# A relative-bias table fetched in two transfers over 128 partitions instead of four over 64

## What is computed

```python
GRID_W = 64; N_HEADS = 16; WIN_ROWS = 8; WIN_COLS = 16     # 128 latent tokens are 2 rows of 64

def na_latent(h, ctx_k, ctx_v, wqkv, wo, rpb):
    ...                                                    # R = 2 grid rows, KR = 2
    row_b = (row_idx - r[:, None]) + (WIN_ROWS - 1)        # key row minus query row: -1, 0, 1
    col_b = jnp.clip(ck[None, :] - cq[:, None] + (WIN_COLS - 1), 0, 2 * WIN_COLS - 2)
    bias = rpb[:, row_b[:, None, :, None], col_b[None, :, None, :]].astype(jnp.float32)
    s_loc = jnp.einsum('brqhd,brkwhd->bhrqkw', q, kg).astype(jnp.float32) * ATTN_SCALE + bias[None]
    s_loc = jnp.where(valid_col[:, None, :], s_loc, -jnp.inf)
    ...                                                    # one softmax with the context scores
```

## Time and profile before

| | us |
|---|---|
| median of 3 runs | 1321.14 |
| lowest, highest | 1320.13, 1322.42 |
| the profiled execution's own time | 1319.5 |
| its span in the trace | 1317.7 |
| busy in the span: PE, DVE, ACT, POOL | 1247.0, 390.7, 330.6, 37.6 |
| moved by DMA | 535.43 MB, 406 GB/s mean |

### The profile page before, as it was taken

The page is one execution under the profiler, slowest core; times in us unless marked ns, Lnnn a source line. Parts: engine busy times, 40 slices in busy tenths (PEclk is TensorE's granted clock), DMA queues, the critical chain, the costliest instruction groups (busy, mean ns, idle before and its releaser), DMA issues.

```text
span 1317.7 us, 17235 instructions
## 1 busy us (share of the span) xinstructions
PE 1247.0 (95%) x6557; PEld 561.7 (43%) x6557; DVE 390.7 (30%) x882; ACT 330.6 (25%) x712; POOL 37.6 (3%) x76
## 2 busy tenths in 40 slices
PE   3979999999899999999999899999999989999996
PEld 0433434343656644443434254443434444434342
DVE  1242213222232324321332324222331452213324
ACT  1241212122221223221212233221222452212122
POOL 2100000000200000000100000000000000000000
PEclk9889999999999999999999999999999999999999
DMA  9999999999999988999999999999999999999994
GB/s 371 420 420 421 421 420 422 421 421 421 400 367 408 394 339 356 422 420 421 421 419 422 421 408 398 422 421 422 420 421 421 413 422 420 422 421 420 422 421 193
DMA packets 87278, 535.43 MB, mean 406 GB/s; under 512 B 11192, under 2 KB 13336, under 8 KB 25760
## 3 DMA queue, kind: packets, MB, share of 16 engines
q1 hardware_dynamic: 82336, 527.47, 97.4%
q0 software_dynamic: 3120, 5.17, 1.2%
q10 hardware_dynamic: 1744, 1.73, 0.4%
HBM read 532.20 MB, written 2.12 MB: 405 GB/s over the span
## 4 chain that ended last, share of the span: by engine, by line
PE 83%; DMA 10%; DVE 3%; ACT 2%; issue 1%; SPq 0%; DVEq 0%; ACTq 0%
PE ps L1954 31%; PE ps L2003 15%; PE ps L1940 5%; PE ps L2015 5%; PE ps L1463 5%; PE ps L1630 4%; PE ps L1592 4%; DMA ring<-in_ada_w_dram 4%; DMA ring<-in_moe_w_up_dram 3%; PE ps L1986 2%; PE ps L1639 2%; DMA ring<-in_attn_wqkv_dram 2%; DMA ring<-in_moe_w_down_dram 2%; PE ps L1560 1%; PE ps L1971 1%; ACT hT L707 1%
## 5 line engine op out<-in xcount | busy, mean ns | idle before, releaser
L1956 PE MATMUL ps<-ring,xg 128*64 128x512 f32 x968 | 438.7, 598 | 0.0
L1954 PE MATMUL ps<-ring,xg 128*64 128x512 f32 x912 | 413.2, 598 | 4.0 <-DMA ring<-in_moe_w_up_dram 4.0
L2003 PE MATMUL ps<-ring,gb 128*64 128x512 f32 x992 | 225.6, 595 | 0.3 <-DMA ring<-in_moe_w_down_dram 0.3
L1954 PEld LDWEIGHTS ps<-ring,xg 128*64 128x64 f32 x912 | 117.7, 137 | 230.0 <-issue 219.6
L1387 DVE SCALAR_TENSOR_TENSOR gb<-ps,gslot,g2x 128x512 f32<-128x512 f32 x128 | 90.2, 746 | 248.8 <-PE ps L2003 248.8
L2003 PEld LDWEIGHTS ps<-ring,gb 128*64 128x64 f32 x992 | 68.9, 137 | 134.2 <-issue 126.2
L1956 PEld LDWEIGHTS ps<-ring,xg 128*64 128x64 f32 x968 | 125.0, 137 | 0.0
L885 ACT ACTIVATE y_hi<-gb 128x512 fp32r<-128x512 f32 x128 | 77.2, 627 | 169.0 <-PE ps L2015 109.1
L1463 PE MATMUL ps<-ring,cact 128*32 128x512 f32 x768 | 94.8, 629 | 12.1 <-ACT cact L668 6.0
L872 ACT ACTIVATE gu<-ps 128x512 f32<-128x512 f32 x64 | 38.3, 598 | 247.0 <-PE ps L1956 247.0
L1396 DVE TENSOR_TENSOR y_lo<-gb,y_hi 128x512 fp32r<-128x512 f32 x128 | 83.6, 688 | 12.5 <-ACT y_hi L885 11.9
(11 more groups left out here) (223 smaller groups left out, 1117.9 us busy)
## 6 DMA issues: line engine op xcount, KB each, us to landing
ring<-in_moe_w_down_dram SPq DMA_DIRECT2D x124, 1024.0 KB, 17.7
ring<-in_moe_w_up_dram SPq DMA_DIRECT2D x121, 1024.0 KB, 16.9
ring<-in_moe_w_gate_dram SPq DMA_DIRECT2D x114, 1024.0 KB, 17.9
ring<-in_ada_w_dram SPq DMA_DIRECT2D x96, 1024.0 KB, 17.9
ring<-in_attn_wqkv_dram SPq DMA_DIRECT2D x12, 1024.0 KB, 21.5
spare<-in_moe_w_down_dram SPq DMA_DIRECT2D x4, 1024.0 KB, 23.6
xh<-in_moe_w_up_dram SPq DMA_DIRECT2D x4, 1024.0 KB, 20.9
hT<-in_moe_w_gate_dram SPq DMA_DIRECT2D x4, 1024.0 KB, 22.7
```

The lines of the kernel that those rows point to most:

```text
L1954: mg = pe.matmul(ps[0:SLOTS, B_GU, :], xg[:, b, e, :], wg[:, i * F:(i + 1) * F], start=(b == 0), stop=(b == DB - 1))
L1956: mu = pe.matmul(ps[SLOTS:P, B_GU, :], xg[:, b, e, :], wu[:, i * F:(i + 1) * F], start=(b == 0), stop=(b == DB - 1))
L2003: mm = pe.matmul(ps[r * SLOTS:(r + 1) * SLOTS, DOWN_BANKS[e % 2], :], acts[:, e % ACTS, j, :], w[:, i * D + r * HALF:i * D + (r + 1) * HAL ...
```

## The change

The table's three parts are stored in reverse order, each by a transfer of its own, so that part `2 - d` of `bias_dram` holds relative row `d`. With that, for a fixed key row the part needed by query row `r` is `1 - kr + r`, which rises with `r`; one source pattern with a leading step of one part (`[P * HEADS, 2]`) covers both query rows. The fetch becomes two transfers over all 128 partitions, 512 KB each. The semaphore's counts follow: the fetch waits for 64 instead of 32, and DVE's wait for 96 stays as it is. The values in `braw` are the same.

```diff
-            pool.dma_start(bias_dram.rearrange("d p h -> p d h"), rback[:, :, :]).then_inc(s_bias, 16)
+            for d in range(3):
+                pool.dma_start(bias_dram[2 - d], rback[:, d, :]).then_inc(s_bias, 16)
...
-            pool.wait_ge(s_bias, 32)
-            for r in range(2):
-                for kr in range(2):
-                    src = bass.AP(tensor=bias_dram.tensor, offset=((kr - r + 1) * P + 1) * HEADS,
-                                  ap=[[HEADS, GRID_W], [1, GRID_W * HEADS]])
-                    pool.dma_start(braw[r * GRID_W:(r + 1) * GRID_W, kr, :, :].rearrange("p k h -> p (k h)"), src).then_inc(s_bias, 16)
+            pool.wait_ge(s_bias, 64)
+            for kr in range(2):
+                src = bass.AP(tensor=bias_dram.tensor, offset=((1 - kr) * P + 1) * HEADS,
+                              ap=[[P * HEADS, 2], [HEADS, GRID_W], [1, GRID_W * HEADS]])
+                pool.dma_start(braw[:, kr, :, :].rearrange("p k h -> p (k h)"), src).then_inc(s_bias, 16)
```

## The result

| | before | after |
|---|---|---|
| median of 4 runs, us | 1320.92 | 1345.72 |
| lowest, highest | 1320.13, 1322.42 | 1343.40, 1347.36 |
| the profiled execution's own time | 1319.5 | 1343.4 |
| its span | 1317.7 | 1341.6 |

The changed kernel is slower by 24.8 us: a ratio of 1.0185, with a 95% interval of 1.0171 to 1.0200. The forecast was 1325.7, and its range ended at 1330.5.

A forecast was written before the change was run, and what follows sets the result against it. The weight stream was taken as the floor of most of the kernel, neck and neck with PE in layer 1's attention. +4.5 us for `qkv 4` and 0.1 for `qkv 1` made +4.6, so 1325.7 us; range 1319.5 to 1330.5.

The forecast's parts named there:

- The direction: Whole kernel: slower, chance 0.69; PE's delay in layer 1's attention moves everything after it by its own size.
- The store and the longer wait: Storing the table in three transfers and waiting for 64 before the fetch: cost nothing.
- two issues fewer: POOL's queue: the `adabr` transfers of `ada 4` are issued 1.1 us earlier, which gives nothing.
- different pairs: Bias fetch: each transfer on two engines, the second on another pair; +4.6 us in sum, chance 0.72.
- 382.3 of my forecast: Bias fetch: the bias lands at 382.3 us, after 64 turns of bias packets alternating with weight packets.
- same pair: Rival for the bias fetch: both transfers on the same two engines, +34 us, 1355 us; chance 0.06.
- cannot tell: `adabr` transfers, outermost count also 2: with only two rows they cannot tell how the changed fetch behaves.
- the landing of `qkv 4`: Its second unit, awaited by PE before V0, lands at 370.8 + 64 q us: 383.6 instead of 379.0, +4.5 us.
- q: Time of one 4 KB bias packet on a two-engine transfer: 0.164 to 0.26 us, taken as 0.20.
- My sign of this step: Stream from 360 to 373 us: less crowded, over 350 GB/s instead of 276.
- The rival on even engines: Bias fetch: all 16 engines share rows, slow packets cured, PE's 1.19 us gap goes; 1319.9 us, chance 0.13.
- both even cases: Bias fetch spread evenly over 16 engines: slow packets cured, 1319.9 us, chance 0.13, or not cured, 1321.1 us, 0.07.

The follow-up runs named there:

- the store alone: Kernel before with the changed kernel's reversed table and three stores, but still its four fetches over 64 partitions: 1320.64 us, ratio 0.9986.
- the kernel by query row: Kernel before with two fetches instead of four, one per query row over 64 partitions, source counting 64, then 2: 1320.70 us, ratio 0.9992.
- the first transfer alone: Changed kernel with only its first bias transfer; the second key row is not fetched and DVE waits for 80 instead of 96: 1330.63 us, ratio 1.0076.
- the other source: Kernel before, four transfers over 64 partitions, but reading non-overlapping 4 KB rows of the two caches instead of the bias table: 1322.51 us in one execution.
- one table: Changed kernel with one 192-column table per key row in HBM, four small stores, source counting 128 rows in one step: 1317.41 us, ratio 0.9969.
- one count of 128: Changed kernel with the source counting 128 rows in one step instead of 2, then 64; bias values not the reference's: 1317.86 us, ratio 0.9970.
- the count of 16: Changed kernel with the source counting 16, then 8, instead of 2, then 64; bias values not the reference's: 1321.44 us in one execution.

## Why the prediction was wrong, point by point

**The direction was right, and so was the argument for it.** The leading 2 confines a transfer to two engines, 64 rows each; `qkv 4` comes late because its slowest engine counts; a gap of PE before L1639 follows; and the delay is kept almost in full to the end (+24.4 at L1630, +23.9 at the end of the span, +24.8 in the medians). The store and the longer wait cost nothing, as the store alone shows, and two issues fewer change nothing either, as the kernel by query row shows.

**The step that failed: "different pairs" taken to mean "in parallel".** I put 0.72 on two pairs that work side by side, with the bias home at 382.3. Two pairs it was, but not side by side. The 14 engines without rows pass 64 empty packets for each transfer, so the second one's pair began some 10 us late and ended at 400.6. The bias came between the 382.3 of my forecast and the 412.0 that I had for one pair, a case with a price of 34 us and a chance of 0.06. And the bias then sets PE's restart: 400.7, plus 3.7 to build it and 4.7 to the end of `normalise(0)`, is 409.1, and `turn(0)` starts at 409.27. The mechanism was open to me only as "same pair"; I gave no case in which two pairs wait for one another. It costs 14.8 of the 24.8 us (1345.72 - 1320.92 against 1330.63 - 1320.60); with an even transfer in its place, 13.3 of them go. I also wrote that the `adabr` transfers "cannot tell" what an outermost 2 does. They say nothing of a long transfer's time, but their 32 packets for two rows showed the empty ones before any run.

**A term that was mis-sized: the landing of `qkv 4`.** The formula gave 383.6 at q = 0.20 and 387.4 at q = 0.26; 387.9 was measured with one transfer and 388.6 with two. I let only the bias packets grow and kept the weight packets at 0.315 and 0.088 us. But the weight packets grew too. The small ones of `qkv 4` did so first: from 366 to 368 us q1's 239 packets, 2.6 KB in the mean, took 93.2% of 32 us, 0.125 us each, where the 352 packets of the earlier trace rows, 2.1 KB in the mean, took 0.091. The large ones followed: from 384 to 400 us q1 had 95.4% of 256 us for 5.44 MB, which is 0.368 us for 8 KB:

```profile
q1 hardware_dynamic: 895, 5.44, 95.4%
```

The earlier trace rows had said it before: there every packet of either queue was one and a half times as long, and I used that for q alone. My sign of this step, over 350 GB/s from 360 to 373 us, was wrong too: 327 from 360 to 373. With the first transfer alone V0 came 8.87 us late against a forecast of 4.5, and 8.87 is above the 8.3 at my upper end.

**A term that was left out: the clock.** After a gap of 10 us or more PE's next 16 matmuls took 8.8 to 9.2 us instead of 7.11. I counted the gap and not what follows it, 1.7 to 2.1 us. Kernels with a short gap have it too: behind 2.27 us (by query row) and 3.10 us (the other source) these matmuls took 8.80; behind 1.19 and 1.43 us they did not.

**The rival on even engines was priced too low.** "The gain is the whole gap of PE and no more", 1.2 us. The two cured kernels gained 3.2 us (one table) and 4.7 us (one count of 128), at nearly the same time, 1317.4 and 1317.9; the medians of before beside them differ. PE's gap of 1.19 us is that small because PE itself was 1.74 us late, through a fall of its clock (0.93 from 340 to 360 us in the earlier trace rows). Where the clock did not fall, the gap of uncured kernels is 2.3 to 3.1 us, and the 1.7 us of slow matmuls come behind it. What a cure gives is read from the landing: V0 starts at 376.16 instead of 379.12.

**What the source and the destination do.** I took the slow packets to come from the destination, because of the earlier trace rows; the other source bears that out. "64 partitions where the others have 128" is not all of it, as the count of 16 shows.

**The range.** It took in both even cases and every q, but of the cases with late bias rows it took none. The cause was that I asked of each resource only how much it must move. For a queue that is served in order one must also ask what stands before the first row.

## What to carry to other kernels

Put a count that 16 divides outermost on both sides of every transfer, at best one count of 128 partitions, and reshape the table in HBM if the pattern doesn't allow it: here that was worth 28 us against the leading 2, and 0.3% against the four transfers over 64 partitions. 16 as the outermost count keeps all engines at work, but only the count of 128 kept the stream at its full rate here. When a transfer on POOL's queue has fewer engines, price it by its longest engine in turns, for itself and for everything queued behind it on every engine. A small gap of PE in one profile is no bound for what a cure gives: read the landing that ends it, and ask why PE was not there earlier.

## What the runs showed of the hardware

- On POOL's queue a transfer on two engines sends to each of the other 14 as many empty packets as each of the two has rows: 1792 for two transfers of 128 rows, 896 for one, 14 for one of two rows. They are cheap (from 358 to 368 us q0 took 9.2% of 160 us; less 41 rows at 0.164 us, that leaves 0.012 us for each of the other 682, and less if the rows took longer; an estimate), but each takes a turn. On ACT's queue the same kind of transfer sent 130 packets in all, which leaves no room for empty ones.
- Each fetch on POOL's queue has 16 packets besides its rows, on ACT's queue this one had 2.
- Beside a fetch whose outermost count is 64 or 16 the packets of the weight stream grow together with the fetch's own: 270 to 292 GB/s in all from 362 to 366 us, against 411 to 415 with the same bytes in one count of 128.
- Landings of transfers that share a semaphore are read off its count. The first transfer of the changed kernel "landed" at 372.1 when its own pair, at four rows a microsecond from 358 us on, had moved fewer than 64 of its 128 rows.
- The PE clock fell near the start of this stretch in some profiled executions (0.91 to 0.93 from 340 to 360 us; in that of before it was 0.50 from 340 to 342, behind gaps of 1.44 and 1.99 us) and not in others (1.00); the changed kernel had the same two gaps and kept 1.00. Where it fell, PE came to the scores 1.7 us later (376.99 against 375.25), and the gap behind them was shorter by that.
